# Odd mixer of a two-block transformer: scores and state outputs from pairs of row halves to one half at a time

## The chip, the cores and the metric

The kernel runs on one core of a Trainium2 chip. The metric is the device time of one execution in microseconds (us); the median of three runs is given.

## The reference: what is computed

Two transformer-like blocks are applied to 512 tokens of width 1024, in f32. The change lies in the second block's odd mixer, which has two parts next to each other: a retention (linear attention with decay) over four heads with keys of width 64 and values of width 128, and a state space model (S5) over 32 groups of 16 channels with 64 complex states. Cut to what matters:

```python
def retention(q, k, v):                      # per chunk of 64 tokens, 4 heads
    scores = jnp.einsum('bnihd,bnjhd->bhnij', qc, kc) * intra_decay
    intra = jnp.einsum('bhnij,bnjhe->bnihe', scores, vc)
    ...
    return (intra + cross).reshape(B_, L, N_HEADS_C, DV_C)

def s5_ssm(u, ...):
    bu = jnp.einsum('gnp,blgp->blgn', b_bar, uf.astype(jnp.complex64))
    a_seq = jnp.broadcast_to(a_bar, bu.shape)
    _, states = lax.associative_scan(_ssm_combine, (a_seq, bu), axis=1)
    y = jnp.einsum('gpn,blgn->blgp', cm, states).real + d_skip * uf
    return y.reshape(B_, L, S5_CH)

def odd_mixer(h, w_in, w_out, ...):
    q, k, v, gate, u = jnp.split(h @ w_in, [...], axis=-1)
    r = rmsnorm(retention(rotary(q), rotary(k), v)) * silu(gate)
    y = gelu(s5_ssm(u, ...))
    ga, gb = jnp.split(y @ glu_w, 2, axis=-1)
    return jnp.concatenate([r, ga * sigmoid(gb)], axis=-1) @ w_out
```

## The kernel before

The kernel is one program with an instruction list for each engine, written out by hand, and semaphores between them (`wait` and `done` with a name and a key). The whole activation stays in SBUF. Each weight matrix is streamed in units of 128 x 1024 numbers through two slots: SP loads a unit, ScalarE copies it to a rounded high part (`split_hi`), VectorE subtracts to get the low part (`split_lo`), and TensorE does three matmuls for each product (L326 to L328 `mm3`). TensorE runs its list in order, so a wait in it holds everything behind.

The odd mixer, `pe_odd`, has units 0 to 15 of the input projection. Unit 14 and 15 are the gates of heads 2 and 3. Between them stand the parts that the change touches:

- `scores(t)` (L2610): for heads 2t and 2t+1, the transposed scores of four key blocks, 64 rows (the key width), widths 512, 384, 256, 128. The even head lies in partitions 0 to 63 and the odd head in 64 to 127 of `o_qk`; the two alternate inside each key block. `ODD_SCORE` gives them banks (2, 3, 6, 3) and (4, 5, 7, 5).
- `decay(h)` on VectorE (L2885): four multiplications by the decay mask out of those banks into `o_w[h % 2]`; signal `decayed`.
- `retain(h)` (L2621): the masked scores times the values, four matmuls, into bank h % 2. ScalarE squares the result for the norm (`heads_square`, L2027), VectorE multiplies it by the gate (`gate_head`, L2892; signal `ret_read`).
- `outputs(half)`: the output of the state space model for 16 groups (8 pairs j, parity `par`). First 16 "direct" matmuls with the taps over 128 rows (L2588), then 32 state matmuls over 64 rows (L2595), into bank 5 for parity 0 and bank 7 for parity 1. Parity 0 reads partitions 0 to 63 and parity 1 reads 64 to 127, in turn. ScalarE copies each bank to `s_y` (`state(u)`, L2773; signal `state_read`).
- `sp_states` on SP's queue: for each half it waits for the half's second `state_read`, stores `s_y` to DRAM in eight pieces, waits, and loads it back in another layout (`o_state`). It stands between the loads of GLU units 1 and 2. VectorE then adds the skip term (`skip(t)`, L2870), ScalarE does `gelu(t)`, and VectorE the low part (`low(t)`, L2875).

After unit 15, `scores(1)`, `retain(2)`, `retain(3)` and the sum of squares over the heads (`heads_sum`, L2037) follow. ScalarE's list has unit 15, gelu(0), gelu(1), the squares of heads 2 and 3, gelu(2), gelu(3), and then the heads' root.

Of the kernel before, what the change touches and what calls it, by code (L numbers as in the profile page):

```python
# [27 lines left out]
P = 128  # L28
S = 512
D = 1024  # L30
KT = D // P
TQ = S // P
# [84 lines left out]
class Signals:  # L117
# [15 lines left out]
    def done(self, ins, name, key=None, by=1):  # L133

        ins.then_inc(self.sem(name), by)
        self.count[name] += by
        if key is not None:
            self.found[name, key] = self.count[name]
# [14 lines left out]
    def wait(self, eng, name, key):  # L153
        eng.wait_ge(self.sem(name), self.at(name, key))


def emit(nc, d, out, known, scratch, skewed, stop=None):

    ctx = ExitStack()
    with ctx:  # L160
        sg = Signals(nc, ctx, known)
        done, loop, mark, at, wait = sg.done, sg.loop, sg.mark, sg.at, sg.wait
# [56 lines left out]
        g = overlay()  # L219
# [4 lines left out]
        g = overlay()  # L224
# [12 lines left out]
        psum = [ctx.enter_context(nc.psum_tensor(f"bank{i}", [P, S], F32)) for i in range(8)]  # L237
# [7 lines left out]
        class Turn:  # L245

            pe = act = dve = sp = 0
# [1046 lines left out]
        g = overlay()  # L1294
# [25 lines left out]
        g = overlay()  # L1320
# [13 lines left out]
        NJ, HOP = 16, 8  # L1334
        BLOCKS = S // HOP
        g = overlay()
        s_taps = place("s_taps", [P, 2 * NJ, P], F32, g)
        s_w = place("s_w", [P, 2 * NJ, P], F32, g)
        s_ca = place("s_ca", [P, 2, NJ, HOP + 1, 16], F32, g)
        s_u = place("s_u", [P, 2 * NJ, BLOCKS], F32, g)  # L1340
        s_s = place("s_s", [P, 2, NJ, BLOCKS], F32, g)
        o_u = place("o_u", [P, TQ, S], F32, g)
        o_qk = place("o_qk", [P, 4, S], F32, g)
        o_rot = place("o_rot", [P, 2, S], F32, g)
        assert g[0] <= group + 8 * NF * S
        g = [group + 8 * NF * S]
# [8 lines left out]
        g = overlay()  # L1355
        s_pt = place("s_pt", [P, NJ // 2, HOP + 1, 16], F32, g)
        s_zero = place("s_zero", [16, P], F32, g)
        g = [group + 16 * NJ * NJ * 4]
        s_q = place("s_q", [P, 2, 2, NJ, BLOCKS - 2], F32, g)
        g = overlay()  # L1360
# [10 lines left out]
        g = [mod_at]  # L1371
# [4 lines left out]
        g = [mod_at]  # L1376
# [947 lines left out]

        ODD_COLS = [3 * S + t * P for t in range(4)] + [t * P for t in range(4)] + [None] * 4 + [2 * S + t * P for t in range(4)]
        ODD_V = (2, 3, 0, 1)
        ODD_SCORE = [[(2, 0), (3, 0), (6, 0), (3, 384)], [(4, 0), (5, 0), (7, 0), (5, 384)]]
        ODD_W = [0, 512, 896, 1152]
        ODD_SPREAD = (4, 6, 7, 3)
        ODD_INPUT = (4, 7)  # L2330
# [170 lines left out]
        def pe_odd(pe, key, after_hidden, squares):  # L2501
# [71 lines left out]
                                               start=c == 0, stop=c == 1, skip_group_check=True)  # L2573
                done(ins, "taps_done", key)

            def outputs(half):

                if half == 0:
                    wait(pe, "taps_loaded", key)
                    wait(pe, "taps_read", key)  # L2580
                    wait(pe, "scanned", key)
                    wait(pe, "decayed", (key, 1))
                else:
                    wait(pe, "state_read", (key, 1))
                for par in range(2):
                    for i in range(8):
                        g = 2 * (8 * half + i) + par
                        nc.tensor.matmul(psum[(5, 7)[par]][:, i * BLOCKS:(i + 1) * BLOCKS], s_taps[:, g, :], s_u[:, g, :],  # L2588
                                         start=True, stop=False, skip_group_check=True)
                for i in range(8):  # L2590
                    j = 8 * half + i
                    for c in range(2):
                        for par in range(2):
                            h = slice(64 * par, 64 * par + 64)
                            ins = nc.tensor.matmul(psum[(5, 7)[par]][:, i * BLOCKS:(i + 1) * BLOCKS],  # L2595
                                                   s_ca[h, c, j, 1:HOP + 1, :].rearrange("p k c -> p (k c)"),
                                                   s_s[h, c, j, :], start=False, stop=c == 1, skip_group_check=True)
                            if i == 7 and c == 1:
                                done(ins, "state_out", (key, 2 * half + par))

            def scores(t):

                if t:
                    wait(pe, "decayed", (key, 1))
                    wait(pe, "state_read", (key, 3))
                for kb in range(TQ):
                    for par in range(2):
                        r = slice(64 * par, 64 * par + 64)
                        bank, c = ODD_SCORE[par][kb]
                        ins = nc.tensor.matmul(psum[bank][:, c:c + S - kb * P], o_qk[r, 2 + t, kb * P:(kb + 1) * P],  # L2610
                                               o_qk[r, t, kb * P:S], start=True, stop=True, skip_group_check=True)
                        if kb == TQ - 1:
                            done(ins, "ret_scores", (key, 2 * t + par))

            def retain(h):
                wait(pe, "decayed", (key, h))
                wait(pe, "proj_read", (key, 12 + h))
                if h >= 2:
                    wait(pe, "ret_read", (key, h - 2))
                for kb in range(TQ):  # L2620
                    ins = nc.tensor.matmul(psum[h % 2][:, kb * P:S], o_v[:, kb, h * P:(h + 1) * P],  # L2621
                                           o_w[h % 2][:, ODD_W[kb]:ODD_W[kb] + S - kb * P], start=kb == 0, stop=kb == TQ - 1,
                                           skip_group_check=True)
                done(ins, "ret_out", (key, h))
# [25 lines left out]
            wait(pe, "values_read", (key, 3))  # L2650
            wait(pe, "taps_read", key)
            scores(0)
            retain(0)
            retain(1)
            outputs(0)
            wait(pe, "ret_read", (key, 0))
            unit(14)
            outputs(1)
            wait(pe, "ret_read", (key, 1))
            unit(15)  # L2660
            scores(1)
            retain(2)
            retain(3)
            heads_sum(pe, key)
# [6 lines left out]
            for n in range(4):  # L2671
                s = unit_ready(pe)
                for m in range(2):
                    bank = 2 * (n % 2) + m
# [4 lines left out]
                    for kt in range(4):  # L2679
                        c = slice(kt * 2 * P + m * P, kt * 2 * P + (m + 1) * P)  # L2680
                        ins = mm3(psum[bank][:, :], w_hi[:, s, c], w_lo[:, s, c], h_hi[:, kt, :], h_lo[:, kt, :], kt == 0,
                                  kt == 3)
# [5 lines left out]
        def act_odd(act, key):  # L2688
# [80 lines left out]
            def state(u):  # L2769
                wait(act, "state_out", (key, u))  # L2770
                half, par = divmod(u, 2)
                groups = s_y[:, NJ * half:NJ * half + NJ, :].rearrange("p (i r) b -> p r i b", r=2)[:, par, :, :]
                done(nc.scalar.activation(groups, psum[(5, 7)[par]][:, :].rearrange("p (i b) -> p i b", i=8), ACT.Copy),  # L2773
                     "state_read", (key, u))
            for u in range(2):
                state(u)
            unit(14)
            for u in range(2, 4):
                state(u)
            unit(15)  # L2780
            gelu(0)
# [24 lines left out]
        def dve_odd(dve, key, after_norm, after_hidden):  # L2806
# [71 lines left out]
            def decay(h):  # L2878
                wait(dve, "ret_scores", (key, h))
                if h >= 2:  # L2880
                    wait(dve, "ret_out", (key, h - 2))
                for kb in range(TQ):
                    bank, at_col = ODD_SCORE[h % 2][kb]
                    n = S - kb * P
                    ins = nc.vector.tensor_tensor(o_w[h % 2][:, ODD_W[kb]:ODD_W[kb] + n], psum[bank][:, at_col:at_col + n],  # L2885
                                                  o_decay[:, h, 0:n], ALU.mult)
                done(ins, "decayed", (key, h))
# [255 lines left out]
```

## Time and profile before

| | |
|---|---|
| median of 3 runs | 3388.02 us (3384.68, 3388.02, 3388.78) |
| the profiled execution | 3388.02 us, of which 3386.2 us span |
| TensorE matmul / weight load busy | 3237.0 us (96%) / 2584.0 us (76%) |
| VectorE, ScalarE, GpSimd busy | 54%, 35%, 29% |
| mean granted TensorE clock | 0.981 |
| last chain | TensorE 83%, VectorE 11%, ScalarE 3% |

The span runs from the first to the last instruction. A matmul's busy time in the profile includes its way through the pipeline, so neighbours overlap; the distance from one start to the next is the better measure of what one costs.

### The profile page before, as it was taken

What the parts mean: (1) busy time and instruction counts of PE and PEld (TensorE: products, weight loads), DVE (VectorE), ACT (ScalarE), POOL (GpSimd) and SP (SyncE); (2) the same over time, 40 slices, a digit from 0 to 9 for tenths busy, and PEclk for the clock granted to TensorE, in tenths of its full rate; (3) what the DMA queues carried; (4) which work ended last, traced back from release to release, by engine and by line L of the source; (5) the groups of instructions that cost most, each with busy time, mean ns of one, the idle gap of its engine ahead of it and who ended that gap; (6) DMA issues with size and microseconds to landing.
All of it is one profiled execution on the core that took longest, in us unless ns stands there. A gap on an engine that the chain in (4) does not pass through costs nothing.

```text
span 3386.2 us, 40313 instructions
## 1 busy us (share of the span) xinstructions
PE 3237.0 (96%) x14573; PEld 2584.0 (76%) x14573; DVE 1812.1 (54%) x2464; ACT 1183.1 (35%) x1782; POOL 997.6 (29%) x722
## 2 busy tenths in 40 slices
PE   6999999999999999999999998999999999899998
PEld 5888866778887888866778887776777777778887
DVE  5454465565445443465655544445776757375443
ACT  3222244432233223344332222454333332343332
POOL 3994000059902800000069800000786000021000
PEclk9999999999999999999999999999999999999999
DMA  6764341157634633321266633212665344243332
GB/s 213 208 206 134 92 130 50 56 168 209 200 96 125 208 95 91 106 66 50 62 188 204 183 96 117 62 44 63 192 200 165 92 119 103 63 129 100 93 93 93
DMA packets 576068, 420.35 MB, mean 124 GB/s; under 512 B 29237, under 2 KB 536196, under 8 KB 574808
## 3 DMA queue, kind: packets, MB, share of 16 engines
q1 hardware_dynamic: 535332, 284.78, 28.6%
q0 software_dynamic: 35456, 124.01, 12.4%
q10 hardware_dynamic: 5172, 10.17, 1.0%
q8 instruction: 62, 1.02, 0.1%
q14 instruction: 46, 0.38, 0.0%
HBM read 413.10 MB, written 8.68 MB: 125 GB/s over the span
## 4 chain that ended last, share of the span: by engine, by line
PE 83%; DVE 11%; ACT 3%; issue 2%; ACTq 0%; DMA 0%; SPq 0%; DVEq 0%
PE bank L326 24%; PE bank L328 24%; PE bank L327 24%; PE bank L1415 2%; PE bank L1443 2%; DVE tmp L451 2%; DVE w_lo L307 2%; DVE h_lo L461 1%; PE bank L1429 1%; PE bank L432 1%; DVE folded L511 1%; DVE w_lo L298 1%; PE bank L358 1%; PE bank L360 1%; PE bank L359 1%
## 5 line engine op out<-in xcount | busy, mean ns | idle before, releaser
L326 PE MATMUL bank<-h_hi,w_hi 128*128 128x512 f32 x2656 | 1056.5, 398 | 55.8 <-DVE h_lo L461 23.1
L328 PE MATMUL bank<-h_hi,w_lo 128*128 128x512 f32 x2656 | 1043.8, 393 | 0.0
L327 PE MATMUL bank<-h_lo,w_hi 128*128 128x512 f32 x2656 | 1043.6, 393 | 0.0
L307 DVE TENSOR_TENSOR w_lo<-raw,w_hi 128x1024 fp32r<-128x1024 f32 x438 | 654.4, 1494 | 580.4 <-ACT w_hi L290 578.6
L290 ACT ACTIVATE w_hi<-raw 128x1024 fp32r<-128x1024 f32 x438 | 462.1, 1055 | 651.5 <-PE bank L328 651.5
L326 PEld LDWEIGHTS bank<-h_hi,w_hi 128*128 128x128 f32 x2656 | 502.4, 189 | 192.3 <-issue 37.8
L328 PEld LDWEIGHTS bank<-h_hi,w_lo 128*128 128x128 f32 x2656 | 503.0, 189 | 108.2
L327 PEld LDWEIGHTS bank<-h_lo,w_hi 128*128 128x128 f32 x2656 | 503.1, 189 | 103.1 <-issue 0.5
L696 POOL TENSOR_TENSOR mod_acc<-mod_acc,mod_w 128x1024 f32<-128x1024 f32 x168 | 430.3, 2562 | 14.6
L326 PE MATMUL bank<-hid_hi,w_hi 128*128 128x512 f32 x1056 | 413.5, 392 | 5.6 <-DVE w_lo L307 5.1
L328 PE MATMUL bank<-hid_hi,w_lo 128*128 128x512 f32 x1056 | 411.7, 390 | 0.0
L327 PE MATMUL bank<-hid_lo,w_hi 128*128 128x512 f32 x1056 | 411.7, 390 | 0.0
L693 POOL TENSOR_SCALAR mod_w<-mod_w,cact 128x1024 f32<-128x1024 f32 x196 | 273.7, 1396 | 8.7
L668 POOL DMA_DIRECT2D mod_w<-in_w_ada x128 | 75.0, 586 | 648.4 <-DVE h_lo L461 611.4
L668 POOL DMA_DIRECT2D mod_w<-in_mod_w x96 | 57.1, 595 | 638.2 <-DVE h_lo L461 606.0
L326 PEld LDWEIGHTS bank<-hid_hi,w_hi 128*128 128x128 f32 x1056 | 198.6, 188 | 49.0 <-DVE w_lo L307 7.3
L328 PEld LDWEIGHTS bank<-hid_hi,w_lo 128*128 128x128 f32 x1056 | 198.6, 188 | 41.8
L327 PEld LDWEIGHTS bank<-hid_lo,w_hi 128*128 128x128 f32 x1056 | 198.5, 188 | 40.7
L298 DVE TENSOR_TENSOR w_lo<-raw,w_hi 128x1024 fp32r<-128x1024 f32 x92 | 112.3, 1223 | 138.8 <-ACT w_hi L281 138.3
L1277 DVE TENSOR_TENSOR hid<-act_t,bank 128x512 f32<-128x512 f32 x127 | 86.9, 684 | 162.8 <-PE bank L328 162.8
L1197 ACT ACTIVATE act_t<-bank 128x512 f32<-128x512 f32 x85 | 50.8, 598 | 315.0 <-PE bank L328 315.0
L1563 POOL DMA_DIRECT2D k_full<-work x16 | 8.0, 510 | 500.1 <-DVE work L1916 500.1
(399 smaller groups left out, 3323.2 us busy)
## 6 DMA issues: line engine op xcount, KB each, us to landing
raw<-in_ffn_w_gu SPq DMA_DIRECT2D x176, 512.0 KB, 4.4
mod_w<-in_w_ada POOLq DMA_DIRECT2D x128, 512.0 KB, 4.0
mod_w<-in_mod_w POOLq DMA_DIRECT2D x96, 512.0 KB, 4.2
raw<-in_ffn_w_in SPq DMA_DIRECT2D x88, 512.0 KB, 3.8
raw<-in_ffn_w_down SPq DMA_DIRECT2D x64, 512.0 KB, 4.1
raw<-in_w_in SPq DMA_DIRECT2D x34, 512.0 KB, 3.7
raw<-in_ffn_w_out SPq DMA_DIRECT2D x32, 512.0 KB, 4.0
raw<-in_ffn_w_down SPq DMA_DIRECT2D x32, 384.0 KB, 3.4
```

Source lines behind the costliest of these rows:

```text
L290: loop(nc.scalar.activation(w_hi[:, u % 2, :], raw[:, u % 2, :], ACT.Copy), "split_hi", times)
L298: done(nc.vector.tensor_tensor(w_lo[:, u % 2, :], raw[:, u % 2, :], w_hi[:, u % 2, :].bitcast(F32), ALU.subtract), "split_lo")
L307: loop(nc.vector.tensor_tensor(w_lo[:, u % 2, :], raw[:, u % 2, :], w_hi[:, u % 2, :].bitcast(F32), ALU.subtract), "split_lo", times)
L326: nc.tensor.matmul(dst, a_hi, b_hi, start=start, stop=False)
L327: nc.tensor.matmul(dst, a_hi, b_lo, start=False, stop=False)
L328: return nc.tensor.matmul(dst, a_lo, b_hi, start=False, stop=stop)
L451: done(nc.vector.scalar_tensor_tensor(tmp[:, m % 3, :], src(m), gain(m), inv, ALU.mult, ALU.mult), "norm_scaled", (key, m))
L668: pool.dma_start(mod_w[:, at_tile % 3, :], src).then_inc(sg.sem(f"mod_loaded{at_tile % 3}"), 16)
L693: done(pool.tensor_scalar(w, w, c, 1.0, ALU.mult, ALU.mult), "mod_step")
L696: done(pool.tensor_tensor(acc, acc, w, ALU.add), "mod_step")
L1277: loop(nc.vector.tensor_tensor(hid[:, jj, :], act_t[:, jj, :], psum[up][:, :], ALU.mult), "pair_evac", times)
L1415: ins = nc.tensor.matmul(psum[bank][:, c:c + n], job["q"](i), job["k"](n), start=True, stop=True, skip_group_check=True)
```

## The change

Scores and state outputs are issued for one row half at a time. `ODD_SCORE` has one set of banks for all heads. `scores(h)` does one head and waits, from the second head on, for the masking of the head before. `outputs(u)` does one parity of one half, its 8 direct matmuls and then its 16 state matmuls. The order on TensorE becomes scores 0, scores 1, retain 0, retain 1, outputs 0, unit 14, outputs 1, 2, 3, unit 15, scores 2, scores 3, retain 2, retain 3. ScalarE reads state 0 before unit 14 and 1 to 3 after it.

```diff
-        ODD_SCORE = [[(2, 0), (3, 0), (6, 0), (3, 384)], [(4, 0), (5, 0), (7, 0), (5, 384)]]
+        ODD_SCORE = [(2, 0), (3, 0), (6, 0), (3, 384)]
...
-            def outputs(half):
-
-                if half == 0:
+            def outputs(u):
+
+                half, par = divmod(u, 2)
+                if u == 0:
                     wait(pe, "taps_loaded", key)
                     wait(pe, "taps_read", key)
                     wait(pe, "scanned", key)
-                    wait(pe, "decayed", (key, 1))
-                else:
-                    wait(pe, "state_read", (key, 1))
-                for par in range(2):
+                if u >= 2:
+                    wait(pe, "state_read", (key, u - 2))
+                h = slice(64 * par, 64 * par + 64)
+                for direct in (True, False):
                     for i in range(8):
-                        g = 2 * (8 * half + i) + par
-                        nc.tensor.matmul(psum[(5, 7)[par]][:, i * BLOCKS:(i + 1) * BLOCKS], s_taps[:, g, :], s_u[:, g, :],
-                                         start=True, stop=False, skip_group_check=True)
-                for i in range(8):
-                    j = 8 * half + i
-                    for c in range(2):
-                        for par in range(2):
-                            h = slice(64 * par, 64 * par + 64)
-                            ins = nc.tensor.matmul(psum[(5, 7)[par]][:, i * BLOCKS:(i + 1) * BLOCKS],
-                                                   s_ca[h, c, j, 1:HOP + 1, :].rearrange("p k c -> p (k c)"),
+                        j = 8 * half + i
+                        dst = psum[(5, 7)[par]][:, i * BLOCKS:(i + 1) * BLOCKS]
+                        if direct:
+                            nc.tensor.matmul(dst, s_taps[:, 2 * j + par, :], s_u[:, 2 * j + par, :], start=True, stop=False,
+                                             skip_group_check=True)
+                            continue
+                        for c in range(2):
+                            ins = nc.tensor.matmul(dst, s_ca[h, c, j, 1:HOP + 1, :].rearrange("p k c -> p (k c)"),
                                                    s_s[h, c, j, :], start=False, stop=c == 1, skip_group_check=True)
-                            if i == 7 and c == 1:
-                                done(ins, "state_out", (key, 2 * half + par))
-
-            def scores(t):
-
-                if t:
-                    wait(pe, "decayed", (key, 1))
-                    wait(pe, "state_read", (key, 3))
+                done(ins, "state_out", (key, u))
+
+            def scores(h):
+                r, t = slice(64 * (h % 2), 64 * (h % 2) + 64), h // 2
+                if h >= 1:
+                    wait(pe, "decayed", (key, h - 1))
                 for kb in range(TQ):
-                    for par in range(2):
-                        r = slice(64 * par, 64 * par + 64)
-                        bank, c = ODD_SCORE[par][kb]
-                        ins = nc.tensor.matmul(psum[bank][:, c:c + S - kb * P], o_qk[r, 2 + t, kb * P:(kb + 1) * P],
-                                               o_qk[r, t, kb * P:S], start=True, stop=True, skip_group_check=True)
-                        if kb == TQ - 1:
-                            done(ins, "ret_scores", (key, 2 * t + par))
+                    bank, c = ODD_SCORE[kb]
+                    ins = nc.tensor.matmul(psum[bank][:, c:c + S - kb * P], o_qk[r, 2 + t, kb * P:(kb + 1) * P],
+                                           o_qk[r, t, kb * P:S], start=True, stop=True, skip_group_check=True)
+                done(ins, "ret_scores", (key, h))
...
             scores(0)
+            scores(1)
             retain(0)
             retain(1)
             outputs(0)
             wait(pe, "ret_read", (key, 0))
             unit(14)
             outputs(1)
+            outputs(2)
+            outputs(3)
             wait(pe, "ret_read", (key, 1))
             unit(15)
-            scores(1)
+            scores(2)
+            scores(3)
             retain(2)
             retain(3)
...
-            for u in range(2):
-                state(u)
+            state(0)
             unit(14)
-            for u in range(2, 4):
+            for u in range(1, 4):
                 state(u)
             unit(15)
...
-                    bank, at_col = ODD_SCORE[h % 2][kb]
+                    bank, at_col = ODD_SCORE[kb]
```

## Rows read from the trace of the kernel before

**Rows 1.** The page: span, and the chain that ended last by engine.

```profile
span 3386.2 us, 40313 instructions
...
PE 83%; DVE 11%; ACT 3%; issue 2%; ACTq 0%; DMA 0%; SPq 0%; DVEq 0%
```

**Rows 2.** Timeline of PE, 2860 to 2908: start, us, line, out<-in, count, idle before.

```profile
2860.65 2.43 PE L2610 MATMUL bank<-o_qk 64*128 64x512 f32 x16
2864.94 6.28 PE L2621 MATMUL bank<-o_w,o_v 128*128 128x512 f32 x16 [1.87 <-DVE o_w L2885]
2871.05 3.68 PE L2588 MATMUL bank<-s_u,s_taps 128*128 128x64 f32 x32
2874.67 3.79 PE L2595 MATMUL bank<-s_s,s_ca 64*128 64x64 f32 x64
2878.39 0.50 PE L326 MATMUL bank<-h_hi,w_hi 128*128 128x512 f32 x1
...
2883.98 3.68 PE L2588 MATMUL bank<-s_u,s_taps 128*128 128x64 f32 x32
...
2896.97 2.43 PE L2610 MATMUL bank<-o_qk 64*128 64x512 f32 x16
2901.53 6.27 PE L2621 MATMUL bank<-o_w,o_v 128*128 128x512 f32 x16 [2.13 <-DVE o_w L2885]
2907.63 3.64 PE L2037 MATMUL bank<-ones,sq 128*128 128x1 f32 x32
```

**Rows 3.** The chain that ended last, 2845 to 2935, in order of time.

```profile
2864.94 6.28 PE bank L2621 x16
2871.22 3.52 PE bank L2588 x32
2874.74 3.72 PE bank L2595 x64
2878.46 0.43 PE bank L326
2878.88 0.23 PE bank L327
```

**Rows 4.** Timeline of DVE, same stretch: masking of the scores and weight splits.

```profile
2863.20 3.27 DVE L2885 TENSOR_TENSOR o_w<-bank,tmp 128x512 f32<-128x512 f32 x8
...
2898.65 1.23 DVE L298 TENSOR_TENSOR w_lo<-raw,w_hi 128x1024 fp32r<-128x1024 f32 x1 [8.76 <-ACT w_hi L281]
2899.80 3.27 DVE L2885 TENSOR_TENSOR o_w<-bank,tmp 128x512 f32<-128x512 f32 x8
```

**Rows 5.** Timeline of PE in the even mixer, 2129 to 2165: scores of single heads.

```profile
2133.93 3.79 PE L1415 MATMUL bank<-e_k,e_q 64*128 64x512 f32 x8 [1.83 <-DVE smx L1480]
...
2151.74 2.42 PE L1415 MATMUL bank<-e_k,e_q 64*128 64x512 f32 x8
2154.10 2.42 PE L1443 MATMUL bank<-e_probs_t,e_v 128*128 128x512 f32 x8
```

**Rows 6.** Timeline of PE: the readout's taps, 64 rows and 16 weight columns.

```profile
2835.21 5.96 PE L2571 MATMUL bank<-s_ca,s_m 64*16 64x128 f32 x128
```

**Rows 7.** Timeline of ACT: the copies of one half's two state banks.

```profile
2878.49 1.09 ACT L2773 ACTIVATE s_y<-bank 128x512 f32<-128x512 f32 x2 [6.63 <-PE bank L2595]
```

**Rows 8.** SP's queue in the second half, and all loads of o_state to landing.

```profile
2892.52 3.81 SPq L2362 DMA_DIRECT2D bias_skewed_rows<-s_y  x8
2897.95 0.38 SPq L2365 DMA_DIRECT2D o_state<-bias_skewed_rows  x1
2898.37 1.91 SPq L271 DMA_DIRECT2D raw<-in_s_glu_w  x2
...
DMA to landing us min/median/max: 3.4/3.7/4.0
```

**Rows 9.** Busy time by stretch: us; PE, PEld, DVE, ACT, POOL; PEclk, DMA, GB/s.

```profile
2861.87:2865.28 3.41, 1.54 (x13) 1.07 (x10) 3.27 (x12) 0.00 (x0) 0.00 (x0) 1.00 1.10 147
2865.00:2871.00 6.00, 6.00 (x16) 3.48 (x17) 3.30 (x6) 1.65 (x2) 0.00 (x0) 0.72 0.56 118
```

## The prediction

> **What bounds the kernel now.** I read the page first: the chain that ended last is 83% TensorE, and no other engine has more than 11% of it [rows 1]. So I looked for the stretch that the edit touches and asked, for each of its TensorE pieces, whether the end of the program hangs on it. The edit touches only the odd mixer, between unit 13 and the sum of squares over the heads, about 2860 to 2908 us. The timeline of TensorE there [rows 2] shows the order of the queue: scores of heads 0 and 1, a gap of 1.87 us, retention of heads 0 and 1, then state outputs, unit 14, state outputs, unit 15, the second scores, a gap of 2.13 us, the second retention. The chain cut to that stretch [rows 3] has the retention, the direct taps and the state matmuls whole. TensorE is never idle between 2864.94 and 2899.4, so what is added to it there is added to the end, unless a wait behind it shrinks. The two gaps end with VectorE's masking of the scores (o_w) [rows 2, 4].
>
> One habit of the trace is needed: each f32 matmul has two records. The 16 score matmuls of four heads would be 32 records, and each pair of heads shows x16; 16 direct taps show x32, 32 state matmuls x64 [rows 2].
>
> **The change part by part.**
>
> *Scores.* Before, a pair of heads runs key block by key block with the head in partitions 0 to 63 and the head in 64 to 127 alternating, in two sets of banks: 16 records in 2.43 us [rows 2]. The even mixer has the same shape for one head alone (64 rows, widths 512 to 128, 8 records): 2.42 us, and from its start to the next group's 2154.10 - 2151.74 = 2.36 us [rows 5]. So the second head costs almost nothing today, and the two halves of the array work at the same time. After the change one head costs 2.36 us and the second follows it.
>
> Where it follows matters more. Both heads now use banks 2, 3 and 6, so the second head's scores wait for the first one's masking. The queue becomes: scores(0) until 2863.0; masking(0) from 2863.20, which is set by the scan on VectorE as before, four of its eight operations, until 2864.9 [rows 4]; scores(1); retention(0) beside masking(1) (1.64 us); retention(1). Retention(0) has the same condition as scores(1) but stands behind it. It starts 2.36 us later. Masking(1), the other half of 3.27 us, takes 1.64 us and is hidden by retention(0), which takes more than 2 us at either clock. (The piece of half clock behind the gap, rival B, now falls on scores(1) instead of retention; it costs the same.) Behind masking(1) on VectorE stand a weight split and two gate products; the split is for unit 15, over 20 us later, and the gates are needed before unit 14, 7 us away. Nobody waits.
>
> The second pair: masking(2) starts 2899.80 because a weight split holds VectorE from 2898.65 for 1.23 us, not because scores are late (they end 2899.40) [rows 2, 4]. With one head's scores of 2.36 us that start stays the same, then scores(3) go between it and retention(2): again 2.36. Two pairs: 2 x 2.36 = **4.7 us**. The gap itself, 1.87 and 2.13 us, stays.
>
> *State outputs.* The direct taps (128 rows, 64 moving columns) are as many as before. They run 32 records in 2874.67 - 2871.05 = 3.62 us, 113 ns each. The state matmuls (64 rows, 64 moving columns, also 128 weight columns) run 64 records in 2878.39 - 2874.67 = 3.72 us, 58 ns each [rows 2]; the other half's taps start 2883.98 and repeat this. Before, they alternate between the halves of the array; after, 16 matmuls in a row use the same half. No row of before shows 64x64 records of one half alone. Bounds: 58 ns if they overlap regardless (nothing lost), 113 ns if two are never in flight, since the tap row is the same form on twice the rows, and for the scores the row of one head (2.36 us) is as long as a row of 128-row matmuls of the same widths (2154.10, 2.42 us) [rows 5]: rows used don't shorten a matmul. I take 113. That is 128 records x (113 - 58) ns = **7.0 us**. At the lower bound it is 0, below 0 is excluded because the same records are issued. In the readout's taps, matmuls of 16 weight columns that change halves only every second matmul run 128 in 5.96 us, 47 ns each [rows 6]; that speaks for some overlap without strict alternation, but there the weights are an eighth as wide and the halves do change.
>
> By the Trainium skill (TensorE: Matmul & The Clock Gate, LDWEIGHTS) a weight load takes its column count over 1.2 GHz whatever the rows, 107 ns for 128 columns, as an estimate. With it the serial state matmuls would add 6.3 us, against 7.0 by the tap row, which I keep.
>
> *More changes between forms.* Before, each half goes taps, states, unit: two changes out of the 64-row form. After there are four such changes. The first matmul behind a state group occupies the chain for 0.43 us (2878.46) where its neighbours take 0.23 [rows 3]: 0.2 us each, two more, **0.4 us**; between nothing and that.
>
> The Trainium skill (TensorEngine Tiling (Array Packing), Key Properties) says that a change of tiling mode drains the engine. Four further changes in both directions would be at most 0.8 us by the same row; the change from taps to states shows no extra time in this trace, so I leave 0.4.
>
> *Placement.* Only the first quarter of the outputs now stands ahead of unit 14, the other three between units 14 and 15. ScalarE reads one bank in half of 1.09 us [rows 7], and each quarter is 5.4 us with a bank of its own per parity, so the bank waits are covered. Weights: unit 15's are ready early. The removed waits (masking(1) and the state reads) had long been met.
>
> What becomes late is the state's way through DRAM: eight stores and a load on SP. From the issue after the last ScalarE read, 2892.52, to the load's issue is 5.4 us, and its landing took up to 4.0: 9.4 us [rows 8]. First half: outputs(0) starts 2871.05 + 2.36 = 2873.4, a quarter is 1.81 + 3.62 = 5.4 plus 0.2, unit 14 takes 2883.98 - 2878.39 = 5.6, so outputs(1) ends 2890.1, is read 2890.8, landed by 2900.2, the skips end 2901.6. Unit 15 ends 2873.4 + 4 x 5.6 + 2 x 5.6 = 2907, masking(2) wants VectorE at 2909.8: cover 8 us. Second half: outputs(3) ends 2901.3, landed by 2911.4; skip(2) stands behind masking(3), which ends 2915.6: cover 4 us. Behind the states SP issues two GLU weight loads, 2898.37 before and about 2908 after, wanted after 2932: covered.
>
> **The sum.** 4.7 + 7.0 + 0.4 = 12.1 us. The profiled execution took 3388.02 us, 3386.2 of it span and 1.8 around it, and is at the median. 3388.0 + 12.1 = **3400.1 us**, slower by 0.36%. A difference under 0.2% (6.8 us) can't be told from none here.
>
> **The rivals.**
>
> *A. State matmuls overlap within one half (not slower).* The place is the state groups: if a record of 64 rows costs 58 ns by itself, for instance because a half load is half the work, the 7.0 falls away and +5.1 remains, 3393.1 us, within 0.2%. It decides below 71 ns a record: 128 x 13 ns = 1.7 us, which is what 5.1 leaves to 6.8. For: the 47 ns of [rows 6]. Against: a single head's scores cost as much as full-height ones [rows 5]. 7%.
>
> *B. More time at the half clock.* The stretch 2865 to 2871 has a granted clock of 0.72, after a 3.41 us stretch in which TensorE was busy for 1.54 [rows 9]; 0.72 over 6 us is 3.4 us at 1.2 GHz of the two levels, each such piece costs 3.4 / 2 = 1.7 us of dense work. Each gap has one piece before, and I keep them. If two more are granted, because scores, gap, scores or the quarter groups with half the array idle count as weak work, it is +15.5: 3403.5 us. For: the one-head row of 3.79 us after a gap of 1.83 [rows 5]. Against: the readout taps run for 6 us on 16 columns at the full 47 ns. 12%. The same mechanism can lose both pieces that follow the gaps, +8.7: 3396.7 us. 8%.
>
> *C. A new wait.* The state's way through DRAM has 4 us of cover. If a wider spread of landings ate 6 us of it, ScalarE's gelu(2) and (3), which stand ahead of the heads' root, would be 2 us late: +14.1, 3402.1 us. 4%.
>
> *D. The change doesn't do what it says*: VectorE already ends both gaps, so serial scores could vanish in them. That would need scores(1) before masking(0); the shared banks forbid it. It would give +7.4, 3395.4 us. 3%.
>
> **How the numbers follow.** Forecast 66%, A 7, B 12 and 8, C 4, D 3. The forecast's own range is 3397.5 to 3403, by the 4 us spread of the three runs. The range 3393.5 to 3405 takes in B, C, D and nearly A. Slower by over 0.2%: all but A and a part of D and B's low side that the runs' spread could pull under 3394.8, 91%; within 0.2%, 8%; faster, 1%, for no case reaches it.
>
> **What the profile after would show.** Right: each score group x8 at 2.4 us, with the gap between the two heads of a pair, and retention directly behind the second; state groups x32 at 3.6 us; retention's end at about 2920 instead of 2907.6, and the rest shifted by the same amount; the span 12 us longer. Wrong: state groups x32 at 1.9 us (A); a granted clock under 1.0 in 2873 to 2907 (B); gelu(2) or the heads' root waiting for a DMA (C). A shift of the rest that differs from that of retention's end by more than 2 us would be clock pieces elsewhere.

## The result, and the profile after

The changed kernel takes 3418.90 us (median of 4 runs, 3414.94 to 3421.58); the kernel before, beside it, 3386.35 (3383.46 to 3388.78). The ratio is 1.0100 with a 95% interval of 1.0088 to 1.0112: about 32 us slower. The forecast was 3400.1 with a range to 3405. The direction was right, the size short by 19 us.

The page of the changed kernel, its span and chain:

```profile
span 3417.6 us, 40311 instructions
...
PE 83%; DVE 11%; ACT 3%; issue 2%; DMA 0%; ACTq 0%; SPq 0%; DVEq 0%
```

The bound is the same [rows 1]. The timeline of TensorE over the edited stretch, the rows that answer to [rows 2]:

```profile
2861.66 2.42 PE L2605 MATMUL bank<-o_qk 64*128 64x512 f32 x8
2865.96 4.63 PE L2605 MATMUL bank<-o_qk 64*128 64x512 f32 x8 [1.87 <-DVE o_w L2882]
2870.52 7.33 PE L2615 MATMUL bank<-o_w,o_v 128*128 128x512 f32 x16
2877.68 1.90 PE L2591 MATMUL bank<-s_u,s_taps 128*128 128x64 f32 x16
2879.51 4.00 PE L2595 MATMUL bank<-s_s,s_ca 64*128 64x64 f32 x32
...
2890.39 1.89 PE L2591 MATMUL bank<-s_u,s_taps 128*128 128x64 f32 x16
2892.21 3.78 PE L2595 MATMUL bank<-s_s,s_ca 64*128 64x64 f32 x32
2895.92 3.09 PE L2591 MATMUL bank<-s_u,s_taps 128*128 128x64 f32 x16
2898.94 7.09 PE L2595 MATMUL bank<-s_s,s_ca 64*128 64x64 f32 x32
2905.96 3.67 PE L2591 MATMUL bank<-s_u,s_taps 128*128 128x64 f32 x16
2909.56 7.09 PE L2595 MATMUL bank<-s_s,s_ca 64*128 64x64 f32 x32
...
2924.07 2.42 PE L2605 MATMUL bank<-o_qk 64*128 64x512 f32 x8
2928.63 4.63 PE L2605 MATMUL bank<-o_qk 64*128 64x512 f32 x8 [2.13 <-DVE o_w L2882]
2933.19 6.72 PE L2615 MATMUL bank<-o_w,o_v 128*128 128x512 f32 x16
2939.75 3.64 PE L2037 MATMUL bank<-ones,sq 128*128 128x1 f32 x32
```

Structure and order are as forecast: scores x8, the same gaps of 1.87 and 2.13 us, retention directly behind the second head. What differs is that equal groups have two lengths: the second quarter of the states takes 2895.92 - 2892.21 = 3.71 us, the third, the same 32 records, 2905.96 - 2898.94 = 7.02; the first head's scores take 2.42, the second's 4.63. The table of stretches (columns as in [rows 9]; PEclk is the first of the last three numbers) says why:

```profile
2861.66:2884.00 22.34, 20.47 (x82) 14.24 (x82) 8.18 (x24) 3.31 (x5) 0.00 (x0) 0.75 0.37 74
2884.00:2890.40 6.40, 6.40 (x25) 5.14 (x24) 0.00 (x0) 0.14 (x1) 0.00 (x0) 0.82 0.00 0
2890.40:2905.90 15.50, 15.50 (x97) 15.19 (x95) 1.47 (x2) 2.14 (x3) 0.00 (x0) 0.70 0.24 69
2905.90:2916.60 10.70, 10.70 (x50) 10.41 (x49) 1.17 (x2) 0.60 (x1) 0.00 (x0) 0.50 0.01 2
2916.60:2924.07 7.47, 7.47 (x25) 5.74 (x24) 0.00 (x0) 0.60 (x1) 0.00 (x0) 0.74 0.32 74
2924.07:2939.75 15.68, 13.55 (x34) 7.86 (x34) 7.03 (x13) 5.23 (x7) 0.00 (x0) 0.67 0.29 99
```

TensorE is busy throughout 2890 to 2924 and yet gets half the clock for most of it, 0.50 over the third and fourth quarters. A stretch of length L at mean clock c has 2 x (1 - c) x L at 1.2 of the two levels 1.2 and 2.4 GHz, here 11.2 + 2.3 + 9.3 + 10.7 + 3.9 + 10.3 = 47.7 us. Before, the same stretch (2860.65 to 2907.63) has two pieces of 3.4, 6.8 us. The excess, 40.9 us, costs about half of itself, 20 us. The stretch is 2939.75 - 2861.66 = 78.1 us long against 47.0, 31.1 more: 20 for the clock and 11 for the work that was forecast at 12.1. Not every half-height group sees the fall: the second quarter, behind unit 14, still runs at the full clock.

### The profile page after: what moved, and what is told of

Read it like the earlier page. It is cut to its first block, busy times and chain, and to the rows that moved or that the text cites. A ratio compares the mean times of both kernels' runs of the same rounds, so it can differ in the third digit from the quotient of the medians.

```text
span 3417.6 us, 40311 instructions
## 1 busy us (share of the span) xinstructions
PE 3269.1 (96%) x14573; PEld 2609.4 (76%) x14573; DVE 1806.4 (53%) x2464; ACT 1182.8 (35%) x1782; POOL 998.3 (29%) x722
## 4 chain that ended last, share of the span: by engine, by line
PE 83%; DVE 11%; ACT 3%; issue 2%; DMA 0%; ACTq 0%; SPq 0%; DVEq 0%
PE bank L326 24%; PE bank L328 24%; PE bank L327 24%; PE bank L1415 2%; DVE tmp L451 2%; PE bank L1443 2%; DVE w_lo L307 2%; DVE h_lo L461 1%; PE bank L1429 1%; PE bank L432 1%; DVE folded L511 1%; PE bank L2595 1%; DVE w_lo L298 1%; PE bank L358 1%; PE bank L360 1%
## 5 line engine op out<-in xcount | busy, mean ns | idle before, releaser
L693 POOL TENSOR_SCALAR mod_w<-mod_w,cact 128x1024 f32<-128x1024 f32 x196 | 277.1, 1414 | 10.2 <-DMA mod_w<-in_mod_w 1.6
```

The source lines that it names most:

```text
L693: done(pool.tensor_scalar(w, w, c, 1.0, ALU.mult, ALU.mult), "mod_step")
```

## The experiments

All times are medians on the chip, with the kernel before run beside each on the same chip (its medians were 3385.89, 3385.97 and 3386.82 us). The interval of each ratio is given as microseconds over before. The ratio is an estimate of its own from all the runs, and its centre can differ by some 3 us from the difference of the two medians, which stands ahead of it. Theory H, formed on the trace above: **the granted clock falls where matmuls that use one half of the rows follow each other.** Height and order were changed apart.

**1. The score part alone.**

```diff
-        ODD_SCORE = [[(2, 0), (3, 0), (6, 0), (3, 384)], [(4, 0), (5, 0), (7, 0), (5, 384)]]
+        ODD_SCORE = [(2, 0), (3, 0), (6, 0), (3, 384)]
...
             scores(0)
+            scores(1)
             retain(0)
...
-            scores(1)
+            scores(2)
+            scores(3)
             retain(2)
```

`scores(h)` is that of the changed kernel, `outputs(half)` that of the one before.

> The kernel before with the score part of the change alone: one head at a time, one set of banks, the state outputs still alternate between the halves of the array. Theory H (the granted clock falls where the matmuls in flight use one half of the rows): 2 x 2.36 = 4.7 us for the work, and the half clock that stands around the two score groups in the changed kernel, 10.2 us each against 3.4 before, costs (10.2 - 3.4) / 2 twice, 6.8 us: +11.5 us. Rival G (the state groups, long and narrow, are what lowers the clock, and score groups only suffer from the gap beside them, as before): +4.7 us and half-clock pieces of 3.4 us after each gap as before.

3396.92 us against 3385.89, +11.0 (ratio 1.0029, +6 to +14). From the first scores of each pair to the end of its retention, in the kernel before:

```profile
2860.65:2871.05 10.40, 8.53 (x33) 5.04 (x33) 7.41 (x23) 2.25 (x3) 0.00 (x0) 0.84 0.77 125
2896.97:2907.63 10.66, 8.53 (x33) 5.21 (x33) 6.94 (x13) 5.23 (x7) 0.00 (x0) 0.84 0.49 154
```

And in this run:

```profile
2861.95:2876.35 14.40, 12.52 (x33) 7.17 (x33) 7.50 (x23) 2.25 (x3) 0.00 (x0) 0.76 0.70 129
2902.25:2916.90 14.65, 12.52 (x33) 7.38 (x33) 7.03 (x13) 5.23 (x7) 0.00 (x0) 0.77 0.35 112
```

Before, 0.84 makes 3.3 and 3.4 us at 1.2 GHz; here 0.76 of 14.4 is 6.9 us and 0.77 of 14.65 is 6.7 us. The state groups, still alternating, have 3.79 us each. The half clock around each pair doubles, where G has it unchanged; G's +4.7 also lies a little below the interval. But H counted 10.2 us for each pair, and here there are 6.8, so the clock costs 3.4 us and not 6.8. The whole stretch takes 2916.90 - 2861.95 = 55.0 us against 47.0, +8.0, which is 4.6 of work and 3.4 of clock. That H's +11.5 meets the median so well is partly luck: 3 us of the +11.0 do not lie in this stretch.

**2. The state part alone.**

```diff
             outputs(0)
             wait(pe, "ret_read", (key, 0))
             unit(14)
             outputs(1)
+            outputs(2)
+            outputs(3)
             wait(pe, "ret_read", (key, 1))
```

`outputs(u)` and ScalarE's order are those of the changed kernel, `scores(t)` and the two sets of banks those of the one before.

> The kernel before with the state part of the change alone: state matmuls of one half at a time, in the places that they have in the changed kernel; scores alternate as before. Theory H: 7.0 + 0.4 us for the work, and the half clock over and around the state groups, 23.9 + 3.4 us in the changed kernel, costs half of itself, 13.7: +21 us. Rival W (the clock falls because serial scores and their waits leave TensorE weak before the outputs begin, and narrow groups only carry it on): the outputs stay at the full clock here, +7.4 us.

3404.46 us, +18.6 (1.0047, +10 to +22). The first retention is unchanged, 6.27 us with its one piece of half clock, and the clock is back up when the outputs begin. The start of the second quarter, and then the rest of the outputs and the start of unit 15:

```profile
2884.05:2887.90 3.85, 3.85 (x35) 3.78 (x34) 1.23 (x1) 1.54 (x2) 0.00 (x0) 1.00 0.02 4
2888.00:2915.00 27.00, 27.00 (x118) 25.83 (x118) 1.41 (x2) 1.79 (x3) 0.00 (x0) 0.50 0.16 45
```

From 1.00 to 0.50 with TensorE never idle between or in them. Rival W falls: the states lower the clock by themselves. 11.0 + 18.6 = 29.6 makes up the whole change within its noise.

**3. The changed kernel with state matmuls of full height.** All 128 partitions of both operands are read, so that both parities' states are summed.

```diff
-                            ins = nc.tensor.matmul(dst, s_ca[h, c, j, 1:HOP + 1, :].rearrange("p k c -> p (k c)"),
-                                                   s_s[h, c, j, :], start=False, stop=c == 1, skip_group_check=True)
+                            ins = nc.tensor.matmul(dst, s_ca[:, c, j, 1:HOP + 1, :].rearrange("p k c -> p (k c)"),
+                                                   s_s[:, c, j, :], start=False, stop=c == 1, skip_group_check=True)
```

> The changed kernel, but each state matmul reads all 128 partitions of both operands instead of 64, so it sums both parities' states (that part of the computation is changed). Counts, order, waits and columns are the same. Theory H: the groups run at 113 ns a record at the full clock, the 27 us of half clock in 2880 to 2920 are gone: 13.7 us less than the changed kernel, +18 us over before. Rival N (matmuls of 64 columns leave the array half idle whatever their height): no difference to the changed kernel, +32 us.

3404.50 us, +18.6 (1.0045, +9 to +21), 14 us under the changed kernel. One quarter in its timeline:

```profile
2890.55 3.74 PE L2595 MATMUL bank<-s_s,s_ca 128*128 128x64 f32 x32
```

And the stretch from the taps of the second quarter to the end of the fourth:

```profile
2888.82:2904.90 16.08, 16.08 (x146) 16.07 (x144) 2.19 (x3) 2.74 (x4) 0.00 (x0) 1.00 0.24 67
```

Same order, same waits, same count, 112 ns a record (2894.12 - 2890.55 for 32) against 116, so as little overlap as in the changed kernel, yet the clock is 1.00 where it was 0.50. This is the run that isolates the cause for the state groups: it is neither the narrow 64 columns nor the missing overlap, but the height. The 18 us of the expectation were met. One thing more differs: at full height no change between the 64-row and the 128-row form is left. Runs 8 and 9 answer that, since they have no more such changes than the kernel before and lose the clock inside a group.

**4. Another placement of the quarters**, two on each side of unit 14.

```diff
             outputs(0)
+            outputs(1)
             wait(pe, "ret_read", (key, 0))
             unit(14)
-            outputs(1)
             outputs(2)
             outputs(3)
...
             state(0)
+            state(1)
             unit(14)
-            for u in range(1, 4):
+            for u in range(2, 4):
                 state(u)
```

> The changed kernel with the second quarter of the outputs moved ahead of unit 14 and its bank read with it, so quarters stand 2 and 2 around unit 14, not 1 and 3. Work and waits the same. Theory H (each stretch of half-height matmuls is enough by itself): between +26 and +32 us over before, since two stretches of 11 us take the place of one of 5.5 and one of 16.5. Rival L (it takes one long run; only the three quarters in a row lower the clock): about 12 us less than the changed kernel, +20 us.

3418.15 us, +32.3 (1.0089, +24 to +36), the same as the changed kernel. The two stretches of outputs:

```profile
2879.99:2896.40 16.41, 16.41 (x99) 15.99 (x97) 0.69 (x1) 1.19 (x2) 0.00 (x0) 0.66 0.00 1
2904.71:2921.90 17.19, 17.19 (x98) 16.77 (x96) 2.55 (x3) 2.14 (x3) 0.00 (x0) 0.63 0.05 18
```

0.66 of 16.4 and 0.63 of 17.2 us are 11.2 and 12.7 at half clock. It doesn't take three quarters in a row; rival L falls.

**5. Scores at full height too.** As run 3, and each score matmul reads both heads' partitions, so that the heads' scores are summed.

```diff
-                    ins = nc.tensor.matmul(psum[bank][:, c:c + S - kb * P], o_qk[r, 2 + t, kb * P:(kb + 1) * P],
-                                           o_qk[r, t, kb * P:S], start=True, stop=True, skip_group_check=True)
+                    ins = nc.tensor.matmul(psum[bank][:, c:c + S - kb * P], o_qk[:, 2 + t, kb * P:(kb + 1) * P],
+                                           o_qk[:, t, kb * P:S], start=True, stop=True, skip_group_check=True)
```

> The changed kernel, but state matmuls and score matmuls read all 128 partitions of both operands (state outputs sum both parities and scores sum both heads: that part of the computation is changed). Counts, order, waits and widths are the same. Theory H (half height lowers the clock): only the work is left, 4.7 + 7.0 + 0.4 = +12.1 us over before, and half-clock pieces of about 3.4 us after each gap, as before. Rival G (around the scores it is the gap and the wait of scores(1), not the height): as the run with the state matmuls alone at 128 rows, +18.6 us.

3394.24 us, +8.3 (1.0024, +5 to +12). From the first quarter to the second scores, and then each pair from its first scores to the end of its retention:

```profile
2870.37:2902.79 32.42, 32.42 (x243) 30.46 (x242) 3.33 (x4) 4.53 (x7) 0.00 (x0) 1.00 0.22 64
2857.87:2870.37 12.50, 10.57 (x33) 6.40 (x32) 7.46 (x23) 2.25 (x3) 0.00 (x0) 0.86 0.69 110
2902.79:2914.01 11.22, 8.89 (x33) 5.52 (x32) 6.93 (x13) 5.24 (x7) 0.00 (x0) 1.00 0.44 143
```

Every wait of the changed kernel is here, and 24 of its 32 us are gone. The gaps of 1.93 and 2.33 us are still there. Rival G (+18.6) falls. The outputs, from the first taps to the second scores with both units, take 32.4 us against 2896.97 - 2871.05 = 25.9 before [rows 2]: +6.5 of work where 7.4 was forecast. The expected +12.1 lies just above the interval; in this execution one gap, not two, is followed by half clock (3.5 us, and 0). Counted in the same way, a pair has 10.1 to 10.4 us of half clock in the changed kernel and in run 4, 6.7 to 6.9 in runs 1 and 3, all with half-height scores of one head at a time, and 3.3 to 3.4 or none in the kernel before and in runs 2 and 6 to 9, where the heads alternate. Around the scores the half height thus adds half clock to what a gap has anyway, which is one piece or none. Whether half-height scores lose the clock without a gap, no run shows.

**6 to 9. How far apart may the halves be?** The kernel before, with only the order of the 32 state matmuls of a group changed: the half is swapped after every 2, 4, 8 or 16 matmuls instead of every one. Waits, banks and scores are as before. The loop for 4 (blocks of 4 and 8 instead of 2 give the swap after 8 and 16; the swap after 2 exchanges the loops over `c` and `par`):

```diff
-                for i in range(8):
+                for i, c, par in [(i, c, par) for b in range(0, 8, 2) for par in range(2)
+                                  for i in range(b, b + 2) for c in range(2)]:
                     j = 8 * half + i
-                    for c in range(2):
-                        for par in range(2):
```

> The kernel before with the two inner loops of the state matmuls swapped: two matmuls in a row use the same half, then two the other. If overlap needs strict alternation: half of the neighbours can still overlap, so a group of 64 records takes between 3.7 and 7.2 us, near 5.5, +3.5 us for both groups. If the queue finds the other half one matmul further on: 3.7 us a group, +0.

> The kernel before with the half swapped after every 4 state matmuls (8 records). Every second matmul already cost nothing. If the queue reaches a fixed number of records ahead and 8 is beyond it: only the two at each seam overlap, groups near 6 us, +4 to +5 us and some half clock; if the reach is longer: groups of 3.8 to 4.5 us, +0 to +1.5 us.

> As the run that swaps every 4, with 8 state matmuls (16 records) on one half before the swap: between the run with 4 and the run with 16, groups of 6 to 7 us and +5 to +10 us if records overlap only near the seam; if a half's whole block of 16 records is reached ahead, near +0.

> The kernel before with one thing changed: in each group of 32 state matmuls the first 16 use one half and the next 16 the other. Waits, banks, places and scores as before. Theory H: 7.0 us of work (64 records a group from 3.7 to 7.2 us), and half clock over much of both groups, now two stretches of 7.2 us: 3 to 7 us more, +10 to +14 us. If the placement and the longer tap-state alternation of the changed kernel are needed for the half clock: +7 us.

| swap after | us | over before (interval) | first, second group, us |
|---|---|---|---|
| 1 (before) | 3386 | 0 | 3.79, 3.79 |
| 2 | 3387.07 | +1.1 (-2 to +4) | 3.84, 3.84 |
| 4 | 3386.43 | -0.4 (-3 to +3) | 4.61, 4.61 |
| 8 | 3396.97 | +10.2 (+6 to +15) | 7.71, 8.94 |
| 16 | 3404.00 | +17.2 (+13 to +24) | 9.31, 9.67 |

The first group of each, in the timelines of the runs with 2, 4, 8 and 16:

```profile
2873.08 3.84 PE L2595 MATMUL bank<-s_s,s_ca 64*128 64x64 f32 x64
```

```profile
2878.89 4.61 PE L2596 MATMUL bank<-s_s,s_ca 64*128 64x64 f32 x64
```

```profile
2872.08 7.71 PE L2596 MATMUL bank<-s_s,s_ca 64*128 64x64 f32 x64
```

```profile
2874.07 9.31 PE L2596 MATMUL bank<-s_s,s_ca 64*128 64x64 f32 x64
```

With 2 in a row nothing is lost, with 4 it is 2883.43 - 2878.89 = 4.54 us for 64 records, 71 ns each, still mostly overlapped. The stretches of the group in the run with 4, and of its start and its middle in the run with 8:

```profile
2878.89:2883.40 4.51, 4.51 (x65) 4.47 (x64) 0.00 (x0) 0.37 (x1) 0.00 (x0) 1.00 0.02 4
```

```profile
2872.08:2876.30 4.22, 4.22 (x47) 4.22 (x46) 0.00 (x0) 0.00 (x0) 0.00 (x0) 1.00 0.00 0
2876.40:2879.70 3.30, 3.30 (x21) 3.20 (x19) 0.00 (x0) 0.60 (x1) 0.00 (x0) 0.51 0.02 5
```

With 8 the start runs at 4.22 us / 46 records = 92 ns, more than halfway from 58 to the serial 116, and then the clock falls. The expectations for 2 and 4 were met on the side of the longer reach. For 8 I had two cases and the one near +0 fell; the other had groups of 6 to 7 us, and they take 7.7 and 8.9. For 16 I gave +10 to +14 and the measured +17.2 has it only at the edge of the interval. The run with 16 is the smallest edit that gives the state part's loss: +17.2 against +18.6 with the quarters moved. So the placement of the quarters costs nothing that these runs can show.

**10. Retention of the first head ahead of the second head's scores.**

```diff
             scores(0)
-            scores(1)
             retain(0)
+            scores(1)
             retain(1)
```

The second pair is changed in the same way.

> The changed kernel with the retention of the first head of each pair ahead of the second head's scores: both wait for the same masking, and the dense 128-row retention then follows the gap. Theory H with order: the work between is the same, but masking(1) is no longer behind a retention, so a second gap of about 1.7 us opens in each pair (+3.4), against up to 3.4 us less half clock: within 4 us of the changed kernel. Rival (the clock around the scores depends only on the score groups being half height): +3 to +5 us over the changed kernel.

3420.22 us, +34.3 (1.0097, +27 to +39); 1 us over the changed kernel, which the two intervals can't separate. The first pair, and the second head's scores of the second pair:

```profile
2862.61 4.12 PE L2615 MATMUL bank<-o_w,o_v 128*128 128x512 f32 x8 [1.87 <-DVE o_w L2882]
2866.66 2.42 PE L2605 MATMUL bank<-o_qk 64*128 64x512 f32 x8
2870.86 2.42 PE L2615 MATMUL bank<-o_w,o_v 128*128 128x512 f32 x8 [1.78 <-DVE o_w L2882]
...
2930.20 2.90 PE L2605 MATMUL bank<-o_qk 64*128 64x512 f32 x8
```

The expected second gap, 1.78 us, is there, and the second head's scores, now behind a retention at full height, run at the full clock in the first pair, 2.42 against 4.63, and mostly so in the second, 2.90. The half clock now falls on the retention behind the gap, 4.12 us where the other one takes 2.42. The gain and the gaps nearly cancel. The run does not decide between its two cases.

**11. An attempt at a better kernel:** before, with the second pair's scores ahead of unit 15, so that VectorE masks them under that unit.

```diff
             outputs(1)
+            scores(1)
             wait(pe, "ret_read", (key, 1))
             unit(15)
-            scores(1)
             retain(2)
...
             skip(1)
-            split_lo(dve)
             decay(2)
             decay(3)
+            split_lo(dve)
```

> The kernel before with the second pair's scores ahead of unit 15 and their masking ahead of the next weight split on VectorE: the gap of 2.13 us and the 3.4 us at half clock behind it (1.7 us) go, a wait of about 1.2 us for ScalarE's reads of the state banks comes: -2.6 us, not clear of noise. Rival (that wait and a later weight split for the GLU cost as much as the gap): 0 to +2 us.

3386.13 us against 3385.97 (1.0005, -1 to +5): no gain. The scores and the second retention:

```profile
2887.50 2.43 PE L2610 MATMUL bank<-o_qk 64*128 64x512 f32 x16 [1.26 <-ACT s_y L2773]
2895.43 4.48 PE L2621 MATMUL bank<-o_w,o_v 128*128 128x512 f32 x16
```

The gap of 2.13 us is gone and a wait of 1.26 us for ScalarE's bank reads stands in its place. The net 0.9 us is below what can be measured.

## Why the prediction was wrong in size

**Right.** TensorE bounds, and everything added there reaches the end. The second head's scores stand on the chain behind VectorE's masking, with the gaps unchanged at 1.87 and 2.13 us. The serial state group: forecast 113 ns a record, measured 3.71 us / 32 = 116 ns at the full clock. Rival A is out: a half-height matmul by itself is no cheaper. Rivals C and D are out: the gap stays in front of scores(1), and the state's way through DRAM stays covered, as the timeline of SP after shows:

```profile
2917.30 3.79 SPq L2362 DMA_DIRECT2D bias_skewed_rows<-s_y  x8
2922.72 0.38 SPq L2365 DMA_DIRECT2D o_state<-bias_skewed_rows  x1
```

With a landing of at most 4 us [rows 8] the data is there by 2927; VectorE's timeline has the skips that read it at 2936.10 (the first half's skips do wait for it, 12.3 us, but end at 2907, with VectorE's next work only at 2925.76):

```profile
2936.10 1.41 DVE L2867 SCALAR_TENSOR_TENSOR o_u<-o_u,cols,o_state 128x512 f32<-128x512 f32 x2
```

**The work.** The terms 4.7 + 7.0 + 0.4 = 12.1 us measured 11 us in the changed kernel's stretch. With full-height operands (run 5), where only work and waits are left, they measured +8.3 (+5 to +12); in its trace the stretch takes 2914.01 - 2857.87 = 56.1 us against 47.0, and as it loses 1.7 us less to the clock than before, the work in it is 10.8. The 0.4 us for changes between forms is too small to be seen by itself. Run 3 has no such change, and its first matmul of a unit behind the states, at the same place in the chain, occupies 0.29 us where [rows 3] has 0.43:

```profile
2883.45 0.29 PE bank L326
```

So of the 0.2 us that I put on a change, 0.14 goes with the form.

**Where it failed.** The step is the sentence "Each gap has one piece before, and I keep them": the sum has nothing for the clock. The size given to rival B, "+15.5", was short in the same way. I took the half clock as something that a gap causes, counted its pieces and carried them over. The changed kernel has 47.7 us of it in the stretch, 27 of them over the outputs and the two units with TensorE never idle: +20 us that no term held. The bound of B, two more pieces, came from nothing in the rows. Two rows were at hand and were read too lightly. The one-head row of 3.79 us after a gap [rows 5] showed half-height scores mostly at half clock: a mean of 0.62 over that row. And the reason I gave against B, that the readout's taps [rows 6] run 6 us on 16 columns at the full clock, speaks of another thing: those matmuls change halves every second time, which is just what the change takes away. (That they overlap is likely from their 47 ns; no run has them on one half.) The run that swaps every second matmul confirms that such an order keeps both overlap and clock.

**Also wrong:** the pieces after the gaps are not fixed. The run that swaps every second matmul has the same gaps as before and no half clock after either; its retention takes 4.58 us instead of 6.28 [rows 2]:

```profile
2865.05 4.58 PE L2621 MATMUL bank<-o_w,o_v 128*128 128x512 f32 x16 [1.87 <-DVE o_w L2885]
...
2900.03 4.58 PE L2621 MATMUL bank<-o_w,o_v 128*128 128x512 f32 x16 [2.13 <-DVE o_w L2885]
```

The runs with 4, 8 and 16 have the piece after the first gap and none after the second, with the same instructions around both. So the order alone doesn't fix them. One trace is kept of each kernel, so it is not shown that they come and go between executions of one kernel; the spread of the kernel before would allow it and is wider than the 4 us of three runs: 3378.57 to 3393.40 over 27 runs.

The share of each cause, in the changed kernel's trace: the first pair of scores with its retention, the outputs with the two units, and the second gap.

```profile
2861.66:2877.68 16.02, 14.15 (x33) 8.17 (x33) 7.48 (x23) 2.25 (x3) 0.00 (x0) 0.68 0.52 104
2877.68:2924.07 46.39, 46.39 (x242) 42.54 (x240) 3.33 (x4) 4.53 (x7) 0.00 (x0) 0.71 0.13 35
2926.49:2928.63 2.14, 0.01 (x2) 0.01 (x1) 2.08 (x5) 2.10 (x4) 0.00 (x0) 0.69 0.50 166
```

The outputs and units have 26.9 us of half clock, which cost 13.5. The two pairs have 10.3 each, 20.6 against 6.8 before; 1.3 of it falls into the gap, where it costs nothing, and half of the rest is 6. The work is what is left of 31.1, 11 us. The runs agree within their noise: for the clock under the states 14 us (the changed kernel against run 3) or 11 (run 2 less its 7.4 of work), for the clock around the scores 6 (run 1 less its 4.7) or 10 (run 3 against run 5, whose traces differ by 5.3 us in the two pairs). What stays open is how the clock is decided; the runs show only which orders of these matmuls keep it.

## What to carry to other kernels

Matmuls that use 64 of 128 rows should alternate between the two halves. For the f32 matmuls measured here, with 128 weight columns and 64 moving columns, a swap after every one or two lets two run in the time of one, a swap after four costs nothing that the times show, and the clock stays up in all three; after eight a part of the overlap is gone and the clock falls. Serial order costs twice, once in time and once in the clock, and here the clock was the larger part (about 20 of 32 us). When a change lowers how much of the array is in use, price its stretch at the half clock as well, even where TensorE is never idle, and make that the upper end of the range.

## What the runs showed of the hardware that I had not expected

- A continuously busy TensorE is granted half its clock when the matmuls in a row use one half of the rows: 0.50 over 27 us in run 2. Not every such group sees it: the second quarter of the changed kernel, behind unit 14, ran at the full clock. With the same order and the full height it keeps 1.00 (run 3, 16 us). Once low, it stayed low through the 128-row taps between the quarters (3.67 us for 16 records that take 1.90 at the full clock) and returned in the dense unit behind.
- Overlap between the halves doesn't need strict alternation: 58 and 59 ns a record with a swap after every 1 and 2 matmuls, 71 with 4, 92 with 8 at the full clock, 116 with one half alone.
- The Trainium skill (TensorE: Matmul & The Clock Gate, HAM oscillation — how this bites in real kernels) ties the fall to the half clock to idle gaps of TensorE between matmuls. These traces show it without a gap, 27 us at 0.50 in run 2 with TensorE busy throughout; the measurement decides.
